# Dilated layer: the heads' steps between the quarters of the projections, queries gathered head by head, the three groups summed by TensorE in its turning

## What is computed

```python
h = x @ b_w_in[0]                                   # 18 query blocks of 128 columns, then 256 for the memory
qd = h[..., 0:2304].reshape(1, 256, 3, 6, 128)      # group g, head h
kv = (x @ shared_w_kv).reshape(1, 256, 2, 6, 128)   # keys and values, shared by the three groups
for g in range(3):                                  # near, every 4th, every 16th key
    s = q[g] @ k.T * 128 ** -0.5, masked for group g
    o[g], lse[g] = softmax(s) @ v, logsumexp(s)
mix = sum over g of softmax(lse over g)[g] * o[g]
mo = softmax(qm @ km.T / 8) @ vm                    # 4 heads of 64, 256 memory rows
y = concatenate([mix, mo]) @ w_out[1]
x = layer_norm(ALPHA * x + y)
```

## Time and profile before

| | us |
|---|---|
| median of 3 runs | 2862.23 |
| lowest, highest | 2860.39, 2867.27 |
| the profiled execution, own time | 2862.17 |
| its span in the trace | 2860.2 |
| projections of this layer, first turning to last matmul | 1018.98 to 1115.50 |
| heads, to the first filler behind them | 1115.50 to 1152.82 |
| turning and output matmuls, to the norm's first filler | 1152.82 to 1178.23 |

### The profile page before, as it was taken

The page is one execution under the profiler, slowest core; times in us unless marked ns, Lnnn a source line. Parts: engine busy times, 40 slices in busy tenths (PEclk is TensorE's granted clock), DMA queues, the critical chain, the costliest instruction groups (busy, mean ns, idle before and its releaser), DMA issues.

```text
span 2860.2 us, 43908 instructions
## 1 busy us (share of the span) xinstructions
PE 2742.7 (96%) x17298; PEld 2407.5 (84%) x17298; DVE 2001.6 (70%) x3889; ACT 1345.8 (47%) x2188; POOL 302.5 (11%) x162
## 2 busy tenths in 40 slices
PE   7999999999999999999999999999999899898997
PEld 7779999998888888799999988888777678786776
DVE  4676988985555655679889755556657759656588
ACT  3423554444445534435454444455235357453465
POOL 0003950000000001049400000000110000000000
PEclk9999999999999999999999999999999999999999
DMA  5344554555665644445544555656421359532586
GB/s 191 113 136 126 177 175 157 155 164 184 195 194 191 223 147 133 142 133 177 170 157 157 167 185 195 194 192 210 125 89 24 125 193 355 185 99 68 174 296 226
DMA packets 175116, 479.04 MB, mean 167 GB/s; under 512 B 27184, under 2 KB 43456, under 8 KB 174912
## 3 DMA queue, kind: packets, MB, share of 16 engines
q1 hardware_dynamic: 171808, 473.29, 50.5%
q10 hardware_dynamic: 3104, 2.95, 0.3%
HBM read 474.61 MB, written 1.57 MB: 166 GB/s over the span
## 4 chain that ended last, share of the span: by engine, by line
PE 87%; DVE 7%; ACT 3%; POOL 2%; issue 1%; DMA 0%; SPq 0%; DVEq 0%; ACTq 0%; POOLq 0%
PE ps L134 86%; POOL ring_rest L154 2%; PE ps L137 2%; DVE spl L154 1%; DVE big L162 1%; ACT big L140 1%; DVE st L178 1%; ACT whi L140 1%; DVE big L154 1%; DVE xb L162 1%; DVE st L162 0%; ACT spl L140 0%; DVE xr L154 0%; POOL big L154 0%; DVE grouped L154 0%
## 5 line engine op out<-in xcount | busy, mean ns | idle before, releaser
L140 ACT ACTIVATE whi<-ring 128x1024 fp32r<-128x1024 f32 x512 | 542.5, 1060 | 686.6 <-PE ps L134 684.7
L134 PE MATMUL ps<-xr,whi 128*128 128x256 f32 x4096 | 750.4, 285 | 11.1 <-POOL ring_rest L154 10.7
L154 DVE TENSOR_TENSOR ring_rest<-ring,whi 128x1024 fp32r<-128x1024 f32 x412 | 503.5, 1222 | 318.1 <-ACT whi L140 318.1
L134 PEld LDWEIGHTS ps<-xr,whi 128*128 128x128 f32 x4096 | 640.4, 193 | 14.0 <-DVE big L184 8.6
L134 PE MATMUL ps<-whi,Ar 128*128 128x512 f32 x2048 | 631.1, 389 | 4.5 <-DVE Ar L154 4.5
L134 PE MATMUL ps<-xr,ring_rest 128*128 128x256 f32 x2048 | 580.8, 284 | 0.0
L154 DVE TENSOR_TENSOR spl<-ring,spl 128x1024 fp32r<-128x1024 f32 (+3 forms) x384 | 435.3, 1163 | 124.9 <-ACT spl L140 115.8
L134 PEld LDWEIGHTS ps<-whi,Ar 128*128 128x128 f32 x2048 | 384.5, 188 | 84.4 <-DVE Ar L154 4.9
L140 ACT ACTIVATE spl<-ring 128x1024 fp32r<-128x1024 f32 (+3 forms) x384 | 373.4, 1008 | 94.5 <-PE ps L134 75.6
L134 PE MATMUL ps<-ring_rest,Ar 128*128 128x512 f32 x1024 | 398.4, 389 | 0.0
L134 PEld LDWEIGHTS ps<-xr,ring_rest 128*128 128x128 f32 x2048 | 394.4, 193 | 0.0
(11 more groups left out here) (127 smaller groups left out, 2488.6 us busy)
## 6 DMA issues: line engine op xcount, KB each, us to landing
ring<-in_peer_u_dram SPq DMA_DIRECT2D x256, 512.0 KB, 3.5
ring<-in_peer_v_dram SPq DMA_DIRECT2D x256, 512.0 KB, 3.5
ring<-in_moe_gate_up_dram SPq DMA_DIRECT2D x128, 512.0 KB, 5.0
ring<-in_moe_w_down_dram SPq DMA_DIRECT2D x64, 512.0 KB, 5.1
ring<-in_peer_w_q_dram SPq DMA_DIRECT2D x32, 512.0 KB, 4.6
ring<-in_sb_w_in_dram SPq DMA_DIRECT2D x24, 512.0 KB, 4.8
ring<-in_ab_w_in_dram SPq DMA_DIRECT2D x20, 512.0 KB, 6.0
ring<-in_w_out_dram SPq DMA_DIRECT2D x16, 512.0 KB, 4.7
```

The lines of the kernel that those rows point to most:

```text
L134: return self.e.matmul(o, l, r, start=start, stop=stop)
L140: return self.e.activation(o, i, f, **k)
L154: return self.e.tensor_tensor(o, a, b, op)
```

## The change

1. The layer's heads run beside the projections. `beside_plan` gives them banks 4 and 5 (scores), 6 (turned), 7 (out); all projections but the second (`Bl`) now have outputs from bank 0 (`base`). The table `B_AT` puts steps 0 to 19 behind quarters 0 or 2 of units 4 to 17; steps 20 to 25 stand in the new `dil_finish`.
2. Memory jobs come first (jobs 0 to 7), dilated jobs are 8 to 19. Keys, memory queries and four heads' values are projected first; `gathered` loads four 128-column pieces so that queries come head by head (three groups of head 0, then head 1, ...). `Bl` and the memory's queries share one projection: nine projections, 18 units, the same matmuls.
3. POOL's adds go. The turning multiplies each group's block by the identity and accumulates the three in PSUM: 3 or 6 plain fp32 matmuls where 1 or 2 transposes stood.
4. The fillers of the heads and of `finish` go, and the `join`s.
5. In `dil_finish` the output weights' order is 3, 0, 1, 2 (`wo1`): the memory's columns of `mix` are turned first.

```diff
-        def projection(name, W, col0, ncols, outs):
+        def projection(name, W, col0, ncols, outs, also=()):
...
+                if also:
+                    gathered((name, g), [(W[d, :], col0, ncols)] + [(X[d, :], c0, n) for X, c0, n in also])
...
+            for s in range(len(jobs)):
+                plan["scores", s] = 4 if total(jobs[s]) > 512 else 4 + s % 2
+                plan["turn", s], plan["out", s] = 6, 7
...
-                    if j.get("sum"):
-                        pe.wait_ge(*gps.at((name, "sum", i)))
...
+                    for g in range(groups if groups > 1 else 0):
+                        ins = pe.matmul(o, Pm(i)[:, g * w + k * 128:g * w + k * 128 + n], ident, g == 0, g == groups - 1)
...
-        out_units("wo1", io["w_out"][1], 0, 1, 2, 3)
+        out_units("wo1", io["w_out"][1], 3, 0, 1, 2)
...
+        for n, p_ in enumerate(projB):
+            p_["base"] = 4 * (n == 1)
...
+        B_AT = [(4, 0), (4, 2), (5, 0), (5, 2), (6, 0), (6, 2), (7, 0), (7, 2), (8, 0), (8, 2), (10, 0), (10, 2),
+                (12, 0), (12, 2), (13, 0), (13, 2), (14, 0), (15, 0), (16, 0), (17, 0)]
...
-            project_all(pe, projB, "x2")
-            psum.close(("end", "B"))
-            busy(pe, 4)
-            join(pe, "B")
-            pe.wait_ge(arrival("kv1"), 16)
-            heads_pe(pe, "dil", jobsB, planB, PTB, PmB, 2, 0)
-            psum.close(("end", "dil"))
+            project_all(pe, projB, "x2", 0, None, dil_beside(pe))
...
+        def dil_finish(e, name, following):
...
+            if e.name == "A":
+                round_unit(e, (name, 0))
+            elif e.name == "V":
+                rest_unit(e, (name, 0))
+            if e.name in "PAV":
+                advance(20)
+                turn_rows(0, 7)
+                out_half(e, name, 0, 0, following)
+                advance(21)
+                out_half(e, name, 0, 1, following)
+                turn_rows(1, 11)
+                advance(22)
+                out_half(e, name, 1, 0, following)
+                advance(23)
+                turn_rows(2, 15)
+                out_half(e, name, 1, 1, following)
+                advance(24)
+                out_half(e, name, 2, 0, following)
+                advance(25)
+                out_half(e, name, 2, 1, following)
+                turn_rows(3, 19)
+                out_both(e, name, 3, following)
```

More of the change, by code:

```diff
@@ L448, in build, with gathered, half, pieces @@
         turns = [0]
-        def projection(name, W, col0, ncols, outs):
+        def gathered(name, parts_of):
+            n = sum(x[2] for x in parts_of)
+            def half(f):
+                return f[:, 0:2 * n].rearrange("p (c n) -> p c n", c=2)
+            def pieces(r, h):
+                v, at, views = half(r), 0, []
+                for W, c0, w in parts_of:
+                    views.append((v[:, :, at:at + w], W[256 * h:256 * h + 256, c0:c0 + w].rearrange("(c p) n -> p c n", p=128)))
+                    at += w
+                return views
+            units[name] = dict(pieces=pieces, half=half)
+        def projection(name, W, col0, ncols, outs, also=()):
             for o in outs:
@@ L560, in heads_pe @@
                 busy(pe, fill if s < 6 else each)
[L561 to L571, removed]
@@ L585, in heads_pe @@
[L585 to L598, removed]
+                heads_step_pe(pe, name, jobs, plan, PT, Pm, s)
@@ L640, in heads_act @@
         def heads_act(act, name, jobs, plan, PT, Pm, Sm, stat):
             for s in range(len(jobs) + 6):
-                if 0 <= s - 4 < len(jobs) and (s - 4) % 2 == 1:
-                    i = s - 4
-                    w = total(jobs[i]) // jobs[i].get("sum", 1)
-                    n, nk = min(128, w), (w + 127) // 128
-                    act.wait_ge(*psum.at((name, "turned", i)))
-                    if i >= 2:
-                        act.wait_ge(*psum.at((name, "out", i - 2)))
-                    act.activation(PT(i)[0:n, 0:nk * 128], bank(plan["turn", i])[0:n, 0:nk * 128], ACT.Copy).then_inc(
-                        *acted.next((name, "copied", i)))
@@ L662, in heads_pool @@
[L662 to L665, removed]
-                w = total(j) // j["sum"]
-                pool.wait_ge(*acted.at((name, "exp", i)))
-                for g in range(1, j["sum"]):
-                    pool.wait_ge(*gps.now())
-                    pool.tensor_tensor(Pm(i)[:, 0:w], Pm(i)[:, 0:w], Pm(i)[:, g * w:(g + 1) * w], ALU.add).then_inc(
-                        *gps.next((name, "sum", i)))
+                heads_step_act(act, name, jobs, plan, PT, Pm, Sm, stat, s)
@@ new lines, in heads_step_act @@
+        def heads_step_act(act, name, jobs, plan, PT, Pm, Sm, stat, s):
+            if 0 <= s - 4 < len(jobs) and (s - 4) % 2 == 1:
+                i = s - 4
+                w = total(jobs[i]) // jobs[i].get("sum", 1)
+                n, nk = min(128, w), (w + 127) // 128
+                act.wait_ge(*psum.at((name, "turned", i)))
+                if i >= 2:
+                    act.wait_ge(*psum.at((name, "out", i - 2)))
+                act.activation(PT(i)[0:n, 0:nk * 128], bank(plan["turn", i])[0:n, 0:nk * 128], ACT.Copy).then_inc(
+                    *acted.next((name, "copied", i)))
+            if 0 <= s - 2 < len(jobs):
+                i = s - 2
+                j, s4, tot = jobs[i], stat(i), total(jobs[i])
+                if i >= 3:
+                    act.wait_ge(*psum.at((name, "turned", i - 3)))
+                act.wait_ge(*vec.at((name, "neg", i)))
+                src = Sm(i) if j["mask"] is not None else bank(plan["scores", i], (tot + 511) // 512)
+                act.activation(Pm(i)[:, 0:tot], src[:, 0:tot], ACT.Exp, bias=s4[:, 1:2],
+                               scale=1.0 if j["mask"] is not None else j["scale"], accum_out=s4[:, 2:3]).then_inc(
+                                   *acted.next((name, "exp", i)))
```

224 lines of the change are left out of this document (132 added, 92 removed).

## The result

The changed kernel takes 2884.22 us (median of 5 runs, 2883.04 to 2896.37) where the kernel before took 2862.23 beside it: ratio 1.0082, 95% interval 1.0060 to 1.0103, so it is slower. The profiled execution took 2883.04, with a span of 2881.3.

The account below looks back on a forecast made before the run. TensorE was taken to bound the kernel. Work 161.2, borders 4.0, steps behind them 4.9, end 10.0 and clock 1.7 gave 181.8 against 159.25: +22.5 us, 2884.7 us, range 2867 to 2894.

Parts of the forecast that it names:

- work without waits: TensorE's own list in the layer's stretch, switches between kinds of matmul included: 161.2 us against 159.25 before.
- the summing: Plain fp32 matmuls replacing transposes in the dilated jobs' turnings add 10.0 us to TensorE's list.
- borders and steps behind them: Waits between projections for the last copy, 4.0 us, and at first steps one quarter behind, 4.9 us.
- waits in the end: Behind the last projection, TensorE waits for rests, stores and turnings among the output matmuls: 10.0 us.
- the clock: Idle behind the last projection lowers TensorE's granted clock: 1.7 us lost, bounds 0 and twice that.
- The switches: 17 changes between kinds of matmul on TensorE in the layer, estimated at 0.1 us each.
- Borders: Next projection's first matmul waits for ACT's last copy: four borders, 3.8 us, with a small rest 4.0.
- Steps behind a border: Outputs wait for bank 7, DVE's store behind its rest: 0.65 at units 8, 10, 12; sum 4.9 us.
- Rival 1: Other engines keep up, so fewer waits in the layer: +10.5 us, chance 0.22; or +2 to +7, chance 0.10.
- Rival 2: Heads' matmuls fill gaps between projection matmuls, steps cost about half: -10 us, 2852; chance 0.04.
- Rival 3: Gathered weight halves land too late from 512-byte runs and four issues per half: +16 us, 2900; chance 0.06.
- The 9.4 worked out as all it could take away: Fillers and waits in the heads' stretch, in the end and ahead of output matmuls: 9.4 us removable.

Follow-up runs that it names:

- best_tsum: `combo_turn` with the groups summed by TensorE again and POOL's adds gone; 2863.74 us, ratio 0.9999 to the kernel before.
- combo_turn: Changed kernel with sums back on POOL, wo1's first unit rounded earlier, steps' places altered, two turned quarters moved earlier; 2855.29 us, ratio 0.9973.
- table: Changed kernel with only the steps' places altered: from unit 5 on none one quarter behind a border; 2875.44 us, ratio 1.0035.
- fill: Changed kernel with 18 filler matmuls on an idle bank in the wait behind the last projection; 2882.19 us, ratio 1.0061.
- early_round: Changed kernel with wo1's first unit rounded and rested during the projections' last unit instead of behind them; 2885.14 us, ratio 1.0062.
- experiments 4 and 5: 4: changed kernel, only steps' places altered, 2875.44 us. 5: kernel before with TensorE's summing alone, 2868.15 us, or 128-column loads alone, 2864.65 us.
- before_tsum: Kernel before with only the summing moved to TensorE's turning and POOL's adds gone; 2868.15 us, ratio 1.0014.
- pool_sum: Changed kernel with POOL adding the three groups again and TensorE turning the sum by transposes; 2880.64 us, ratio 1.0052.

## Why the prediction was right, point by point

Forecast 2884.7, measured 2884.22; stretch forecast 181.8, measured 182.05. The mechanism is the one forecast. That the sums agree this closely is luck: in the stretch, two terms forecast 1.0 and 0.8 too high offset two forecast 0.9 and 0.5 too low and 0.65 that no term has, and in the time, runs of the same kernel lie up to 13 us apart, with the profiled execution 2.5 us shorter ahead of the layer. The terms, with what the runs isolate:

| term | forecast | measured | by |
|---|---|---|---|
| work without waits | 161.2 | 160.2 | `best_tsum`: 161.66 - 1.07 - 0.42 |
| of it the summing | 10.0 | 10.16 | `best_tsum` less `combo_turn` |
| borders and steps behind them | 4.0 + 4.9 | 9.8 | after less `table` |
| waits in the end | 10.0 | 9.2 | brackets of after: 4.08, 1.50, 1.67, 0.42, 1.51 |
| the clock | 1.7 | 2.2 | starts of after less `fill` (2.15) and `early_round` (2.25) |
| sum | 181.8 | 181.4 | the stretch is 182.05; 0.65 unassigned |

The 0.65 is of the size of the hidden part of the waits in the end (their brackets leave out some 0.15 to 0.25 each, experiments 4 and 5); it was not isolated.

- **Work.** Within 1 us, for reasons that cancel. The pair of dilated jobs between quarters takes 4.39 us by starts in `best_tsum` (1125.50 to 1127.51 and 1129.84 to 1132.22), less than 4.64 (the scores of 256 columns: six records in 1.11, where twice 0.11 each was 1.32), so six pairs are 1.5 under the forecast. The switches were put at 0.1 each: 18 projection matmuls ahead of a step take 1129.84 - 1127.51 = 2.33 where 18 x 0.120 = 2.16, and some places show less. The two leave 0.5 unexplained.
- **Borders.** Idle of 0.68 three times, 0.93 by starts: the 0.94 of the earlier trace rows. The fourth shows 0.52 released by what the profile calls issue; ACT's copy of the last output ends 0.10 us ahead of that start (1145.38 + 0.38, start 1145.86), so it may be the same wait, which stays open.
- **Steps behind a border.** Forecast 0.65 at units 8, 10, 12: brackets of 0.54, and 0.38 more ahead of the scores at unit 10 only. Unit 6: 0.9 against 0.77. Unit 14: 1.5 against 1.26. Unit 16: 0.5 against 0.52. The mechanism is the one named, DVE's rest ahead of its store, and `table` ends it. One reading was a little short: by the earlier trace rows the rest is over 2.89 us behind the projection (2515.40 + 1.23 - 2513.74), not 2.8, which would have made 0.65 some 0.75.
- **The end.** TensorE's gap behind the last projection was to be 4.3 (from 1155.47 + 12 x 0.120 = 1156.9, the end of the projection by prices): 4.40. Behind it 1.57, 1.85, 0.7 and 1.57 became 1.50, 1.67, 0.42 and 1.51. `early_round` removes the first alone, `combo_turn` 1.67 and the last 1.51, and takes 0.43 off the 1.50.
- **Clock.** 2.2 where 1.7 stood, within the bounds of 0 and 3.4: the row taken from the norm had 2.58 us of idle ahead of it, here it is 4.08, and more work fell to the lower level.
- **Rival 1** (ACT and DVE keep up) is out: eleven waits within the projections, eight of them released by DVE's store or ACT's copy. That the order and not the engines' share of work did it is shown by `table`, which gives them no less work.
- **Rival 2** (gaps filled) is out: +10.16 for 54 matmuls is their full price. The 0.2 that six records of 256 columns take less by starts (1.11 for 1.32) comes back in the projection matmuls behind them (2.33 for 2.16).
- **Rival 3** (loads late) is out. The page of after, part 6:

```profile
ring<-in_b_w_in_dram SPq DMA_DIRECT2D x72, 128.0 KB, 2.7
```

2.7 us to landing where 9.1 was the bound from the earlier trace rows, and no wait of ACT's rounding for them reached TensorE. The rule of 512-byte runs from the page "DMA: Bandwidth & Descriptors" of the Trainium skill, cited for rival 3, is not contradicted: 128 KB in such runs landed in 2.7 us and nothing waited. Whether that is full rate was not measured.

What the forecast did not see: the change's idea holds when the places are better. Waits and clock were 21.9 us of the stretch's 182.05 (182.05 - 160.2), and summing 10.2 of the rest; with 1.5 us of waits left and the sum on POOL the same change wins 7.75 us. The 9.4 worked out as all it could take away is what `combo_turn` nears.

## What to carry to other kernels

- Moving attention steps between the quarters of a matmul-bound projection pays only what they leave behind as idle (here 7.75 of 9.4 us), and costs it back at once when a step stands one quarter behind a projection's border: put such a step, whose bank is freed by an engine that also serves the border, at the border itself or two quarters (24 matmuls, 2.9 us) and more behind it, as `table` does. Read it from the waits of TensorE by releaser, and from the next engine's list: a long operation (here a rest of 1.2 us, or two) ahead of the short one that frees a single bank is the defect.
- When TensorE is the bound, a wait for another engine is weighed against the work that would replace it: 10.2 us of summing stood for 2.9 us of waits for POOL, about 4 by starts (10.0 - 6.1, `before_tsum`); with more distance in the pipeline those waits vanish by themselves, as in `pool_sum` and all its descendants.
- A bracket's idle is a lower end for what a wait costs; take the distance of starts. Here a wait of 4 us of TensorE also cost 2.2 us by its clock.

## What the hardware showed beyond that

- Idle in brackets was 7.1 us for eleven waits whose removal gave 9.8; the same 0.25 a wait fits `combo_turn` (3.6 of brackets and 2 waits gone, 4.15 measured). The six waits for POOL hid 0.15 each, and the one of 4.08 hid 0.16 (4.24 by starts).
- With the same code, the first 24 projection matmuls behind a norm's wait took 2.97 us in one execution (after) and 4.41 in another (`early_round`, granted clock 0.63). Stretches are compared only with that looked at.
